# The first block of the input projection: GpSimd's weight remainders start after VectorE's scaling, and the block's products run in three passes

## The chip, the core and the metric

The kernel runs on one core of a Trainium2 chip. The metric is the device time of one execution in microseconds, as the median of the runs. The kernel before takes 1242.05 us (3 runs, 1239.67 to 1242.12).

Five engines work side by side, each through its own list of instructions: TensorE (PE in the profile, its weight loads PEld), VectorE (DVE), ScalarE (ACT), GpSimd (POOL) and SyncE (SP), which here issues most of the DMAs. They wait for each other through semaphores.

## The reference, cut to what matters

One layer of a hybrid backbone runs over 128 context tokens and 256 latent tokens (384 in all). What bears on this case is its start: the modulated RMSNorm and the input projection.

```
h = rmsnorm(x, lp['norm1_w']) * (1 + sc1) + sh1        # (384, 1024); sc1, sh1 from silu(cond) @ w_ada
proj = h @ lp['w_in']                                  # 1024 -> 6496 columns, float32
z_s, xbc, dt_s, qkv, z_d, a_d, b_d = jnp.split(proj, list(np.cumsum(cuts)), axis=-1)
xbc = jax.nn.silu(centred_dwconv(xbc, lp['conv_ssd_w'], lp['conv_ssd_b']))
... # SSD scan, gated delta rule scan, output projection, gated residual
x = x + gt2 * hier_moe(h, lp)                          # 32 experts, top-2 of the top-1 group
```

## The kernel before, in words

Activations lie transposed: `h1_t` holds 8 slices (k = 0 to 7) of 128 features by 392 columns, 384 tokens and 8 columns of padding for the convolution. `KD` is 8.

The projection is made in 50 blocks of 128 output columns. To keep float32 precision, a factor is split in a high part (rounded to fp32r, `w_hi` and `h1_hi`) and a remainder (`w_lo`, `h1_lo`), and a block is the sum of three products for each of 8 slices: w_hi x h1_hi, w_lo x h1_hi, w_hi x h1_lo, 24 matmuls in all.

Who makes what, each engine in the order of its own list:

- ScalarE: `hi_part(n)` (L1122) rounds the weights of block n into `w_split[:, n % 4, 0]`. It makes those of blocks 0, 1 and 2 (`AHEAD` is 3), then the eight slices of `h1_hi` (L1129), each after VectorE has scaled that slice; afterwards the weights of block n + 3 when block n is done.
- GpSimd: for each block, the remainder of the weights, `w_split[:, n % 4, 1]` = weights - `w_hi` (L522), as soon as ScalarE has made the high part.
- VectorE: scales and shifts `h1_t` in place, 16 instructions (L1398: for each slice one of 128 columns, the context tokens, and one of 256, the latent ones), then makes the eight slices of `h1_lo` (L1402) from `h1_t` and `h1_hi`, and then goes on with the convolution of each block that is done (L1410, L1412).
- TensorE: block 0 waits for its weight remainder (`split_ready`) and then, slice by slice, for `h1_lo` (`h1_ready`); each slice has its three matmuls behind each other (L651). Blocks 1 to 49 follow with no wait inside.

The order of the instructions on an engine is the order in which the Python code issues them; there is no scheduler. The weights of block 0 to 3 come by one DMA into the tile `mix`, those of later blocks in halves of `ring_a`. In the profile's names, `kv` is `h1_t` at this point, `h_hi` and `h_lo` are `h1_hi` and `h1_lo`, and `ps` is PSUM. Behind the projection come the scans, the output projection and 16 pairs of experts, whose weight loads SyncE issues when earlier products are done.

Of the kernel before, what the change touches and what calls it, by code (L numbers as in the profile page):

```python
# [7 lines left out]
KD = D_MODEL // P  # L8
# [4 lines left out]
ROW = TOK + 8  # L13
# [46 lines left out]
def hybrid_step(nc, x_t, xs_t, pos_t, params, masks, w_ada, w_in, w_out, h0_ssd, s0_dn, router, final_rows, w_gate, w_up, w_down,  # L60
# [5 lines left out]
    with ctx:  # L66
# [58 lines left out]
        ps = ctx.enter_context(nc.psum_tensor("ps", [P, 8, 512], fp32))  # L125
# [34 lines left out]
        blocks = []  # L160
        for n, (a, w) in enumerate(proj_cols):
            for b in range(w // P):
                i = len(blocks)
# [31 lines left out]
        h1_full = sem("h1_full")  # L195
        h1_hi_ready = sem("h1_hi_ready")
        h1_ready = sem("h1_ready")
        hi_ready = sem("hi_ready")
        split_ready = sem("split_ready")
        block_mm = sem("block_mm")  # L200
# [316 lines left out]
        @block.gpsimd  # L517
        def _(pool):

            for n, (load, c, kind, i) in enumerate(blocks):  # L520
                pool.wait_ge(hi_ready, n + 1)
                nc.gpsimd.tensor_tensor(w_split[:, n % 4, 1, :, :], slots[slot_of[load]][:, :, c:c + P],  # L522
                                        w_split[:, n % 4, 0, :, :].bitcast(fp32), ALU.subtract).then_inc(split_ready, 1)
# [74 lines left out]
        def _(pe):  # L598
# [26 lines left out]
            for k in range(KD):  # L625
                last = nc.tensor.matmul(ps[:, 1, 0:TOK], mask("ones"), v_t[:, k, :], start=(k == 0), stop=(k == KD - 1))
# [10 lines left out]
                nc.tensor.matmul(ps[:, i % 2, 0:TOK], mask("ones"), sq[:, i % 2, :], start=True, stop=True).then_inc(qk_sum, 1)  # L637


            for n, (load, c, kind, i) in enumerate(blocks):  # L640
                pe.wait_ge(split_ready, n + 1)
                if 3 <= n < CONV_BLOCKS + 3:
                    pe.wait_ge(conv_done, n - 2)
                elif n >= 3:
                    pe.wait_ge(block_out, n - 2 - CONV_BLOCKS)
                w_hi, w_lo = w_split[:, n % 4, 0, :, :], w_split[:, n % 4, 1, :, :]
                for k in range(KD):
                    if n == 0:
                        pe.wait_ge(h1_ready, k + 1)
                    for x, (w, h) in enumerate(((w_hi, h1_hi), (w_lo, h1_hi), (w_hi, h1_lo))):  # L650
                        last = nc.tensor.matmul(ps[:, 2 + n % 3, 0:ROW], w[:, k, :], h[:, k, :],  # L651
                                                start=(k == 0 and x == 0), stop=(k == KD - 1 and x == 2))
                last.then_inc(block_mm, 1)
                if n == 9:
                    pe.wait_ge(masks_in, 32)

                    pe.wait_ge(wab_in, 32)
                    for t in range(TT):
                        for k in range(KD):
                            at = ROW_SEGS[min(t, 1)][0] + max(t - 1, 0) * P  # L660
                            last = nc.tensor.matmul(ps[:, 5, 64 * t:64 * t + 64], h1_t[:, k, at:at + P],
                                                    w_ab[:, k, :], start=(k == 0), stop=(k == KD - 1))
                    last.then_inc(tok_mm, 1)
                if kind == "z" and i == 3:

                    pe.wait_ge(log_ready, 1)
                    half_ones = {"first64": mask("ones64")[:, 0:1].to_broadcast([P, P]), "last64": mask("ones64")[:, P - 1:P].to_broadcast([P, P])}
                    for t in range(TT):
                        for m, a, b, o in (("upper", 0, 16, 0), ("lower", 16, 32, 16), ("upper64", 32, 40, 32), ("lower64", 40, 48, 40),
                                           ("ones", 0, 32, 48), ("ones64", 32, 48, 80), ("first64", 32, 48, 96), ("last64", 32, 48, 112)):  # L670
                            last = nc.tensor.matmul(ps[:, 6, t * P + o:t * P + o + b - a], half_ones[m] if m in half_ones else mask(m), g_log[:, t, a:b], start=True, stop=True)
                    last.then_inc(cum_mm, 1)
                if kind == "z" and i:
                    norm_sum(i - 1)
# [92 lines left out]
            for t in range(TT):  # L767
# [4 lines left out]
                for i, src in enumerate((k_t, v_t)):  # L772
                    for b in range(KD):
                        last = nc.tensor.transpose(ps[:, 2 * i + b // 4, (b % 4) * P:(b % 4 + 1) * P], src[:, b, t * P:(t + 1) * P], mask("ident"))
# [122 lines left out]
            for n in range(13):  # L897
# [3 lines left out]
                elif n == 4:  # L901

                    pe.wait_ge(sq_ready, 2)
                    for k in range(KD):
                        last = nc.tensor.matmul(ps[:, 6, 0:TOK], mask("ones"), y_sq[:, k, :], start=(k == 0), stop=(k == KD - 1))
# [63 lines left out]
            for n, k in enumerate((0, 4, 1, 5, 2, 6, 3, 7)):  # L969
                pe.wait_ge(h2_ready[k // 4], k % 4 + 1)  # L970
                for t in range(TT):
                    last = nc.tensor.matmul(ps[:, 5 + t, 0:N_ROUTE], h2_t[:, k, t * P:(t + 1) * P], router_sb[:, k, :],
                                            start=(n == 0), stop=(n == KD - 1))
# [115 lines left out]
        def _(act):  # L1089
# [28 lines left out]
            def hi_part(n):  # L1118
                load, c = blocks[n][:2]
                if c == 0:  # L1120
                    act.wait_ge(slot_in[slot_of[load]], 16 * arrivals(load))
                nc.scalar.copy(w_split[:, n % 4, 0, :, :], slots[slot_of[load]][:, :, c:c + P]).then_inc(hi_ready, 1)  # L1122

            AHEAD = 3
            for n in range(AHEAD):
                hi_part(n)
            for k in range(KD):
                act.wait_ge(h1_full, k + 1)
                nc.scalar.copy(h1_hi[:, k, :], h1_t[:, k, :]).then_inc(h1_hi_ready, 1)  # L1129


            def norm(i):
# [801 lines left out]
```

## Time and profile before

| what | value |
|---|---|
| time, median of 3 runs | 1242.05 us (1239.67 to 1242.12) |
| the profiled execution's own time | 1238.15 us |
| its span | 1236.3 us |
| TensorE busy in the span | 91% |
| VectorE, ScalarE, GpSimd busy | 45%, 24%, 19% |
| mean granted TensorE clock | 0.951 of full |

The span runs from the first to the last instruction. TensorE is busy nearly all the time, with a gap of 12.4 us ahead of the projection's first block. Busy TensorE is not TensorE at full speed: the granted clock counts too (1.00 is 2.4 GHz, 0.50 is 1.2 GHz).

### The profile page before, as it was taken

What the parts mean: (1) busy time and instruction counts of PE and PEld (TensorE: products, weight loads), DVE (VectorE), ACT (ScalarE), POOL (GpSimd) and SP (SyncE); (2) the same over time, 40 slices, a digit from 0 to 9 for tenths busy, and PEclk for the clock granted to TensorE, in tenths of its full rate; (3) what the DMA queues carried; (4) which work ended last, traced back from release to release, by engine and by line L of the source; (5) the groups of instructions that cost most, each with busy time, mean ns of one, the idle gap of its engine ahead of it and who ended that gap; (6) DMA issues with size and microseconds to landing.
All of it is one profiled execution on the core that took longest, in us unless ns stands there. A gap on an engine that the chain in (4) does not pass through costs nothing.

```text
span 1236.3 us, 21464 instructions
## 1 busy us (share of the span) xinstructions
PE 1121.7 (91%) x8981; PEld 736.6 (60%) x8981; DVE 551.6 (45%) x1062; ACT 300.7 (24%) x640; POOL 232.0 (19%) x179
## 2 busy tenths in 40 slices
PE   3599999998697889999899789999999999999996
PEld 1499999997454589999655575333333333333332
DVE  1776776333985356567510341333333222222223
ACT  2333334346221223555200122000000000000002
POOL 0354555341132122222000101000000000000000
PEclk9799999898896999999999759999999999999999
DMA  9632333225024420010400446999999999999993
GB/s 363 216 137 69 136 137 129 75 71 219 18 91 187 171 71 3 4 38 4 154 1 1 202 189 273 425 423 425 426 426 427 424 425 426 425 426 424 424 425 126
DMA packets 52460, 279.20 MB, mean 226 GB/s; under 512 B 6529, under 2 KB 13953, under 8 KB 32929
## 3 DMA queue, kind: packets, MB, share of 16 engines
q1 hardware_dynamic: 49136, 271.66, 54.4%
q0 software_dynamic: 3248, 6.45, 1.5%
q8 instruction: 59, 0.97, 0.3%
q14 instruction: 17, 0.13, 0.0%
HBM read 278.61 MB, written 4.72 MB: 229 GB/s over the span
## 4 chain that ended last, share of the span: by engine, by line
PE 71%; DMA 15%; DVE 9%; ACT 3%; issue 1%; SPq 0%; DVEq 0%; ACTq 0%
PE ps L651 18%; DMA ring_b<-in_w_up 15%; PE ps L1024 14%; PE ps L892 7%; PE ps L1040 5%; PE ps L1054 4%; PE ps L818 3%; PE ps L830 2%; PE ps L827 2%; PE ps L608 2%; DVE temp L1513 1%; DVE temp L1494 1%; PE ps L721 1%; PE ps L741 1%; PE ps L750 1%
## 5 line engine op out<-in xcount | busy, mean ns | idle before, releaser
L651 PE MATMUL ps<-h_hi,w_split 128*128 128x392 f32 x800 | 214.4, 349 | 12.4 <-DVE h_lo L1402 12.4
L651 PEld LDWEIGHTS ps<-h_hi,w_split 128*128 128x128 f32 x800 | 148.5, 190 | 16.7 <-issue 13.2
L651 PE MATMUL ps<-h_lo,w_split 128*128 128x392 f32 x400 | 137.3, 343 | 0.0
L522 POOL TENSOR_TENSOR w_split<-ring_a,w_split 128x1024 fp32r<-128x1024 f32 x46 | 110.8, 2408 | 107.4 <-ACT w_split L1122 107.4
L1040 PE MATMUL ps<-mix,temp 128*64 128x512 f32 x256 | 112.8, 594 | 13.6 <-ACT temp L1343 13.6
L1024 PE MATMUL ps<-ring_b,temp 128*64 128x512 f32 x512 | 113.1, 593 | 7.0 <-DMA ring_b<-in_w_up 7.0
L1024 PE MATMUL ps<-ring_a,temp 128*64 128x512 f32 x512 | 113.4, 595 | 1.2 <-ACT temp L1335 1.2
L1040 PE MATMUL ps<-kv,temp 128*64 128x512 f32 x256 | 113.3, 595 | 0.0
L1054 PE MATMUL ps<-temp 128*128 128x512 f32 x192 | 92.8, 619 | 0.0
L1024 PEld LDWEIGHTS ps<-ring_b,temp 128*64 128x64 f32 x512 | 40.4, 137 | 78.4 <-issue 78.4
L1412 DVE SCALAR_TENSOR_TENSOR temp<-ps,pc,temp 128x388 f32<-128x388 f32 x136 | 84.6, 622 | 4.8
L1024 PEld LDWEIGHTS ps<-ring_a,temp 128*64 128x64 f32 x512 | 35.8, 137 | 76.2 <-issue 76.2
L1122 ACT CAST w_split<-ring_a 128x1024 fp32r<-128x1024 f32 x46 | 48.3, 1049 | 132.4 <-PE ps L651 132.4
L1339 ACT ACTIVATE temp<-ps 128x512 f32<-128x512 f32 x16 | 9.6, 597 | 289.7 <-PE ps L1024 289.7
L1040 PEld LDWEIGHTS ps<-mix,temp 128*64 128x64 f32 x256 | 33.7, 137 | 74.1 <-issue 73.2
L1805 DVE TENSOR_TENSOR x_ssd<-x_ssd,ps 128x512 f32<-128x512 f32 x96 | 66.0, 687 | 25.6 <-PE ps L1054 25.6
L579 POOL DMA_INDIRECT temp<-h_rows,cur_tok x16 | 29.6, 1852 | 247.4 <-PE ps L1014 246.5
L651 PEld LDWEIGHTS ps<-h_lo,w_split 128*128 128x128 f32 x400 | 75.9, 190 | 0.0
L556 POOL TENSOR_TENSOR temp<-bc,masks_sb 128x256 f32<-128x256 f32 x60 | 45.6, 776 | 119.6 <-DVE bc L1563 72.5
L1054 PEld LDWEIGHTS ps<-temp 128*128 128x128 f32 x192 | 29.9, 188 | 62.7 <-DVE x_ssd L1805 41.4
L1796 DVE TENSOR_TENSOR temp<-ps,temp 128x512 f32<-128x512 f32 x32 | 22.1, 692 | 96.6 <-PE ps L1040 96.6
L1578 DVE TENSOR_TENSOR temp<-temp,ps 128x512 f32<-128x512 f32 (+1 forms) x60 | 38.0, 634 | 54.6 <-PE ps L830 54.2
(280 smaller groups left out, 1595.7 us busy)
## 6 DMA issues: line engine op xcount, KB each, us to landing
ring_a<-in_w_gate SPq DMA_DIRECT2D x32, 2048.0 KB, 15.4
ring_b<-in_w_up SPq DMA_DIRECT2D x32, 2048.0 KB, 18.3
kv<-in_w_down SPq DMA_DIRECT2D x32, 1024.0 KB, 21.2
mix<-in_w_down SPq DMA_DIRECT2D x32, 1024.0 KB, 19.2
ring_a<-in_w_in SPq DMA_DIRECT2D x11, 2048.0 KB, 7.7
ring_a<-in_w_ada SPq DMA_DIRECT2D x6, 2048.0 KB, 9.8
ring_b<-in_w_ada SPq DMA_DIRECT2D x6, 2048.0 KB, 18.3
ring_a<-in_w_out SPq DMA_DIRECT2D x2, 2048.0 KB, 14.3
```

Of the source, the lines that this page charges most:

```text
L522: nc.gpsimd.tensor_tensor(w_split[:, n % 4, 1, :, :], slots[slot_of[load]][:, :, c:c + P], w_split[:, n % 4, 0, :, :].bitcast(fp32), ALU.s ...
L556: nc.gpsimd.tensor_tensor(dn_off[a][lev % 2], dn_m[a], mask(f"lev{par}_{LEVELS[lev]}").unsqueeze(1).to_broadcast([P, 4, DN_CHUNK]), ALU.mu ...
L651: last = nc.tensor.matmul(ps[:, 2 + n % 3, 0:ROW], w[:, k, :], h[:, k, :], start=(k == 0 and x == 0), stop=(k == KD - 1 and x == 2))
L818: last = nc.tensor.matmul(A[rows, h, :], off[rows, h, :], mask("eye")[rows, :] if lev == 0 else d[rows, h, :], start=True, stop=True, tile ...
L892: last = nc.tensor.matmul(ps[:, 4 + b % 4, 0:TOK], slots[slot_of[load]][:, k % KD, (b % 4) * P:(b % 4 + 1) * P], mix[:, k, :], start=(k == ...
L1024: last = nc.tensor.matmul(ps[64 * e:64 * e + 64, 2 + n, :], xg_t[:, k, 64 * e:64 * e + 64], slots[2 * n + e][:, k, :], start=(k == 0), sto ...
L1040: last = nc.tensor.matmul(ps[64 * e:64 * e + 64, 5 + n, :], e_act_t[:, f, 64 * e:64 * e + 64], down[4 + e][:, f, n * 512:(n + 1) * 512], s ...
L1054: nc.tensor.matmul(ps[:, (7, 4)[m % 2], :], sel_t[:, t * P:(t + 1) * P], e_y[:, n * 512:(n + 1) * 512], start=True, stop=True).then_inc(sp ...
L1122: nc.scalar.copy(w_split[:, n % 4, 0, :, :], slots[slot_of[load]][:, :, c:c + P]).then_inc(hi_ready, 1)
L1412: ins = V.scalar_tensor_tensor(c_acc, row[:, j:j + W5], col("conv_w", CONV_W * i + j), c_acc, ALU.mult, ALU.add)
L1578: V.tensor_tensor(dn_dd[a][g][:, at:512], dn_dd[a][g][:, at:512], ps[:, a, at:512], ALU.subtract).then_inc(d_ready[a], 1)
L1805: V.tensor_tensor(a, a, ps[:, (7, 4)[m % 2], :], ALU.add).then_inc(acc_added, 1)
```

## The change

Three edits, all around block 0:

1. GpSimd waits for `h1_full` at 8, which VectorE reaches when the last slice is scaled, ahead of its first weight remainder.
2. ScalarE makes `h1_hi` slices 0 to 3, then the high weights of block 0, then slices 4 to 7, then the high weights of blocks 1 and 2.
3. TensorE takes block 0 in three passes over the slices: w_hi x h1_hi, then w_hi x h1_lo, then w_lo x h1_hi. A pass waits for each slice of what it reads (`h1_hi_ready` or `h1_ready`), and the third waits for the remainder of the weights.

```
@@ -517,6 +517,7 @@
         @block.gpsimd
         def _(pool):
 
+            pool.wait_ge(h1_full, KD)
             for n, (load, c, kind, i) in enumerate(blocks):
                 pool.wait_ge(hi_ready, n + 1)
                 nc.gpsimd.tensor_tensor(w_split[:, n % 4, 1, :, :], slots[slot_of[load]][:, :, c:c + P],
@@ -637,7 +638,18 @@
-            for n, (load, c, kind, i) in enumerate(blocks):
+            def first_block():
+                pe.wait_ge(hi_ready, 1)
+                for x, (w, h, made) in enumerate(((0, h1_hi, h1_hi_ready), (0, h1_lo, h1_ready), (1, h1_hi, h1_hi_ready))):
+                    if w:
+                        pe.wait_ge(split_ready, 1)
+                    for k in range(KD):
+                        pe.wait_ge(made, k + 1)
+                        last = nc.tensor.matmul(ps[:, 2, 0:ROW], w_split[:, 0, w, k, :], h[:, k, :], start=(x == 0 and k == 0), stop=(x == 2 and k == KD - 1))
+                last.then_inc(block_mm, 1)
+
+            first_block()
+            for n, (load, c, kind, i) in list(enumerate(blocks))[1:]:
                 pe.wait_ge(split_ready, n + 1)
...
                 for k in range(KD):
-                    if n == 0:
-                        pe.wait_ge(h1_ready, k + 1)
                     for x, (w, h) in enumerate(((w_hi, h1_hi), (w_lo, h1_hi), (w_hi, h1_lo))):
...
             AHEAD = 3
-            for n in range(AHEAD):
-                hi_part(n)
             for k in range(KD):
+                if k == KD // 2:
+                    hi_part(0)
                 act.wait_ge(h1_full, k + 1)
                 nc.scalar.copy(h1_hi[:, k, :], h1_t[:, k, :]).then_inc(h1_hi_ready, 1)
+            for n in range(1, AHEAD):
+                hi_part(n)
```

ScalarE's list from the copy of the modulation row out of PSUM to the first convolved block, before:

```order
L1104 COPY temp<-ps 128x512
L1122 CAST w_split<-mix 128x1024 x3
L1129 CAST h_hi<-kv 128x392 x8
L1122 CAST w_split<-mix 128x1024
L1122 CAST w_split<-ring_a 128x1024
```

And the same stretch of ScalarE's list now (lines shifted; L1132 is the weights, L1139 the activations):

```order
L1114 COPY temp<-ps 128x512
L1139 CAST h_hi<-kv 128x392 x4
L1132 CAST w_split<-mix 128x1024
L1139 CAST h_hi<-kv 128x392 x4
L1132 CAST w_split<-mix 128x1024 x3
L1132 CAST w_split<-ring_a 128x1024
```

Two of the three early weight blocks moved behind all of `h_hi`, and the first one between its halves. The third `mix` cast in the last group of three is that of block 3, which waits for block 0 as before.

TensorE's list with its waits, from the modulation's transposes over the first two slices of block 0, before:

```order
L619 MATMUL ps<-masks_sb,temp 128x128 x3
L651 MATMUL ps<-h_hi,w_split 128x392 [waits h1_ready,split_ready]
L651 MATMUL ps<-h_hi,w_split 128x392
L651 MATMUL ps<-h_lo,w_split 128x392
L651 MATMUL ps<-h_hi,w_split 128x392 [waits h1_ready]
L651 MATMUL ps<-h_hi,w_split 128x392
L651 MATMUL ps<-h_lo,w_split 128x392
```

And now, the whole of block 0 and the start of block 1:

```order
L620 MATMUL ps<-masks_sb,temp 128x128 x3
L648 MATMUL ps<-h_hi,w_split 128x392 [waits h1_hi_ready,hi_ready]
L648 MATMUL ps<-h_hi,w_split 128x392 [waits h1_hi_ready] x7
L648 MATMUL ps<-h_lo,w_split 128x392 [waits h1_ready] x8
L648 MATMUL ps<-h_hi,w_split 128x392 [waits h1_hi_ready,split_ready]
L648 MATMUL ps<-h_hi,w_split 128x392 [waits h1_hi_ready] x7
L661 MATMUL ps<-h_hi,w_split 128x392 [waits split_ready]
```

The 24 matmuls are the same; the wait for the weights' remainder moved behind sixteen of them, and the wait for `h_lo` behind eight.

## Rows read from the trace of the kernel before

**Rows 1.** Chain that ended last, from 34 to 100 us: start us, us, what.
```profile
35.70 0.67 PE ps L619 x4
...
36.97 11.17 DVE kv L1398 x16
48.14 0.48 DVE h_lo L1402
48.62 0.14 issue
48.76 45.02 PE ps L651 x240
```

**Rows 2.** Busy time and granted clock (PEclk) of three stretches, DMA share second last.
```profile
36.97:39.20 2.23, 0.00 (x0) 0.00 (x0) 2.23 (x8) 0.85 (x1) 0.00 (x0) 1.00 1.01 396
...
48.76:52.80 4.04, 4.04 (x12) 4.04 (x13) 3.19 (x7) 0.00 (x0) 0.00 (x0) 0.50 0.41 128
...
59.32:93.70 34.38, 34.38 (x195) 34.38 (x194) 25.37 (x40) 13.93 (x25) 19.32 (x8) 1.00 0.36 123
```

**Rows 3.** VectorE's scaling line: before 39.4 us, 39.6 to 46.8 us, and last three; ns.
```profile
L1398 DVE TENSOR_SCALAR kv<-kv,amp,mod x9: 339/347/409, 37.0 to 39.3; 128x128 f32<-128x128 f32 x5, 128x256 f32<-128x256 f32 x4
...
L1398 DVE TENSOR_SCALAR kv<-kv,amp,mod x4: 339/2509/2580, 39.3 to 44.4; 128x128 f32<-128x128 f32 x2, 128x256 f32<-128x256 f32 x2
...
L1398 DVE TENSOR_SCALAR kv<-kv,amp,mod x3: 335/402/404, 47.2 to 47.7; 128x256 f32<-128x256 f32 x2, 128x128 f32<-128x128 f32 x1
```

**Rows 4.** Timeline, VectorE then GpSimd, around 39.5 us; GpSimd's weight line later.
```profile
39.54 2.58 DVE L1398 TENSOR_SCALAR kv<-kv,amp,mod 128x256 f32<-128x256 f32 x1
...
39.48 7.34 POOL L522 TENSOR_TENSOR w_split<-mix,w_split 128x1024 fp32r<-128x1024 f32 x3 [39.02 <-ACT w_split L1122]
...
L522 POOL TENSOR_TENSOR w_split<-mix,w_split x1: 2413/2413/2413, 56.4 to 56.4; 128x1024 fp32r<-128x1024 f32 x1
```

**Rows 5.** ScalarE's timeline, 15 to 60 us, and VectorE's low parts by line.
```profile
38.35 2.94 ACT L1122 CAST w_split<-mix 128x1024 fp32r<-128x1024 f32 x3 [2.70 <-DMA mix<-in_w_in]
41.20 2.19 ACT L1129 CAST h_hi<-kv 128x392 fp32r<-128x392 f32 x5
...
L1402 DVE TENSOR_TENSOR h_lo<-kv,h_hi x8: 551/552/553, 48.1 to 51.4; 128x392 fp32r<-128x392 f32 x8
```

**Rows 6.** VectorE and GpSimd at 216 to 225 us, and line 1427 later.
```profile
218.10 1.39 DVE L1427 SCALAR_TENSOR_TENSOR q_t<-q_t,temp 128x384 f32<-128x384 f32 x1 [1.78 <-ACT temp L1100]
...
223.03 1.33 DVE L1427 SCALAR_TENSOR_TENSOR q_t<-q_t,temp 128x384 f32<-128x384 f32 x1 [3.06 <-ACT temp L1100]
...
216.68 2.40 POOL L522 TENSOR_TENSOR w_split<-ring_a,w_split 128x1024 fp32r<-128x1024 f32 x1 [2.53 <-ACT w_split L1122]
221.60 2.35 POOL L522 TENSOR_TENSOR w_split<-ring_a,w_split 128x1024 fp32r<-128x1024 f32 x1 [2.52 <-ACT w_split L1122]
...
L1427 DVE SCALAR_TENSOR_TENSOR kv<-kv,temp x8: 557/558/1380, 266.1 to 292.0; 128x384 f32<-128x384 f32 x8
```

**Rows 7.** VectorE's run of L1513 at 340 us, and GpSimd's instruction that began within it.
```profile
340.18 2.44 DVE L1513 SCALAR_TENSOR_TENSOR temp<-temp,gates 128x128 f32<-128x128 f32 x1
...
339.89 2.58 POOL L540 TENSOR_TENSOR temp<-temp,bc 64x1024 f32<-64x1024 f32 x1 [6.56 <-ACT temp L1202]
```

**Rows 8.** VectorE and GpSimd at 698 to 702 us, both with work ready.
```profile
698.28 2.58 DVE L1695 TENSOR_TENSOR buf_h<-q_t,temp 128x1536 f32<-128x1536 f32 x1 [2.80 <-ACT temp L1100]
700.90 0.90 DVE L1698 TENSOR_SCALAR buf_h<-buf_h,amp,mod 128x128 f32<-128x128 f32 x1
...
698.25 0.99 POOL L575 TENSOR_TENSOR buf_h<-q_t,temp 128x384 f32<-128x384 f32 x1 [114.19 <-ACT temp L1100]
699.21 2.51 POOL L575 TENSOR_TENSOR buf_h<-q_t,temp 128x384 f32<-128x384 f32 x1
701.67 0.99 POOL L575 TENSOR_TENSOR buf_h<-q_t,temp 128x384 f32<-128x384 f32 x1
```

**Rows 9.** TensorE's timeline in block 0, and block 1's first pair.
```profile
49.55 0.53 PE L651 MATMUL ps<-h_lo,w_split 128*128 128x392 f32 x1
...
50.53 0.53 PE L651 MATMUL ps<-h_lo,w_split 128*128 128x392 f32 x1
...
53.79 0.34 PE L651 MATMUL ps<-h_lo,w_split 128*128 128x392 f32 x1
...
54.32 0.34 PE L651 MATMUL ps<-h_lo,w_split 128*128 128x392 f32 x1
...
55.04 0.52 PE L651 MATMUL ps<-h_hi,w_split 128*128 128x392 f32 x2
```

## Prediction

> **What bounds the kernel now.** I read the page first for the gap ahead of the projection, then the chain of waits from 34 to 100 us, then the timelines of VectorE, GpSimd and ScalarE in that stretch, and last the places later in the trace where VectorE and GpSimd work at once. The chain [rows 1] shows the whole start of the projection: TensorE ends its transposes at 36.4, then VectorE's sixteen scalings hold the chain for 11.17 us, one `h_lo` follows, and block 0 starts at 48.76. From there to 93.8 TensorE runs 240 matmuls without a gap. So a microsecond taken from ahead of block 1 should be a microsecond of the total: all later work starts from TensorE's progress, and the weight loads are issued on that progress too.
>
> The scalings have two speeds. Nine of them take 339 to 409 ns; three take about 2.5 us, 2.58 the longest; behind these they are at 335 to 404 again [rows 3]. The tenth starts at 39.54 [rows 4], so nine pitches are 2.57 us, 0.286 each. The three slow ones lie exactly over GpSimd's three weight remainders, 39.48 to 46.82 [rows 4]. GpSimd is held hardly at all: 7.34 us for three, and one alone takes 2.41. The two engines exclude each other for a whole instruction, and take turns: one scaling gets in at each change of GpSimd's instruction. Of the 11.17 us about 6.5 are this.
>
> **The change, part by part.** *GpSimd waits.* The scalings then run at their own pitch: the last ends at 36.97 + 15 x 0.286 + 0.40 = 41.66, against 48.14. That is 6.5 us, and nothing else on VectorE moves. If this arrived at block 1 the kernel would gain 6.5 us.
>
> *ScalarE's order.* `h_hi` 0 to 3 follow the scalings (a slice every 0.58) and end near 39.9. One weight cast is 1.04 us and three are 2.94, a pitch of 0.95; five `h_hi` are 2.19 us, a pitch of 0.42 [rows 5]. So `hi_part(0)` ends near 40.9 and its weights had landed by 38.35 [rows 5]; `h_hi` 7 needs the last scaling and ends near 42.5; `hi_part(1)` and `hi_part(2)` end near 43.5 and 44.5. None of these is late for what follows.
>
> *GpSimd's remainders move on to `h_lo`.* This is the step that decides. GpSimd's first remainder now begins at about 41.75, the moment VectorE begins the eight `h_lo`. These take 0.552 us each at a pitch of 0.48 when alone [rows 5], and they read two tensors in SBUF. The trace shows what such an instruction does beside GpSimd: at 218.10 one of 384 columns took 1.39 us and ended 0.41 after GpSimd's instruction (216.68 + 2.40 = 219.08); at 223.03 again, 1.33 us, 0.41 behind 223.95; with GpSimd idle the same form takes 0.557 [rows 6]. A run of them does not keep GpSimd out: at 340.18, in the middle of eight, one took 2.44 us because a GpSimd instruction had begun at 339.89 [rows 7]. And where both have work ready they alternate strictly: GpSimd's at 699.21 took 2.51 instead of 0.99, ending 0.86 after the VectorE instruction (700.86), the next VectorE one ended only at 701.80, and so on [rows 8].
>
> With these numbers: `h_lo` 0 runs 41.59 to 42.14. GpSimd's first remainder, pending, ends about 2.33 later (2.41 alone, less the start already behind it; bounds 2.27 and 2.41), at 44.47; `h_lo` 1 ends 0.42 later, 44.89; second remainder 47.22, `h_lo` 2 47.64; third 49.97, `h_lo` 3 50.39. GpSimd has no fourth until block 0 is done. `h_lo` 4 to 7 follow at 0.477: 52.30. In the trace before only the first `h_lo` was on the path, 0.48 us [rows 1]; now all eight are, for 52.30 - 41.66 = 10.6 us. The 6.5 us that the scaling gives back are taken by `h_lo`, and more.
>
> The Trainium skill has this rule in "SBUF — State Buffer", section "Who interferes with whom": a VectorE instruction with two SBUF inputs contends with a GpSimd one that reads SBUF, although it has no two-port mode, and the later one blocks for the whole instruction. Rows 6 to 8 agree (1.39 against 0.557 us). [...]
>
> *TensorE's three passes.* Alone among the edits this one earns something: in the trace before, all 24 matmuls stand behind `h_lo` 0 and the first remainder; now eight (w_hi x h1_hi) run from about 41 to 43.7, and of the second pass seven run as `h_lo` comes. Behind `h_lo` 7 nine are left: its own and the third pass. The matmuls have two paces: at the granted clock 0.50, the 1.2 GHz level [rows 2], three take 0.98 us (49.55 to 50.53), 0.327 each; at 1.00, 2.4 GHz, three take 0.53, 0.178 each [rows 9]. The first nine after 52.30 + 0.14 (the issue gap, rows 1) = 52.45 take 1.60 us at the higher level and 2.94 at the lower: block 1 would start between 54.05 and 55.4. Before it starts at 55.04 [rows 9]. So the sum for block 1's start is -1.0 to +0.35.
>
> *The clock.* TensorE stood at 0.50 from 48.76 to 52.8 after 12 idle us, and rose after 4.0 us of dense work [rows 2]. Now it has eight matmuls at 41, then one in almost 3 us until 50.4, and dense work from 50.5 (70% busy) or 52.45. If it rises 4.0 us after 50.5, at 54.5, block 1 starts at 52.45 + 9 x 0.178 + 6.3 x 0.149 = 55.0, no change; if it rises 4.0 after 52.45, block 1 starts at 55.4 and about 3 more matmuls cost 0.149 extra, together +0.9. The bounds of this term are -1.0 (never low after 52.45) and +0.9; I take the middle of the two cases with rows behind them, +0.4 us.
>
> *Cover.* The remainders of blocks 1 and 2, now ready at 47.2 and 50.0, are needed at 55 and 59: 5 us to spare. The DMA's share fell from 1.01 to 0.41 ahead of 52.8 [rows 2], so the next weights have landed. Later, GpSimd's remainders meet VectorE's convolution, which has one operand in PSUM, as before. No DMA is moved, and SyncE's waits are the same.
>
> **Sum,** to block 1's start: scaling -6.5; `h_lo` on the path 10.6 instead of 0.5, +10.2; block 0's matmuls on the path 6.3 us before (48.76 to 55.04) and 1.6 to 2.9 now, -4.7 to -3.4; low matmuls behind that, 0 to +0.5. Together -1.0 to +0.9, taken as +0.4, on an execution of 1238.15 us (span 1236.3). The median of the runs is 1242.05, 0.3% above that execution; the difference carries over: 1242.4 us. About 0.2%, 2.5 us, is what a measurement of this kernel can tell from none, so the forecast is no change.
>
> **Rivals.** *A: `h_lo` isn't held.* If these eight, with output in fp32r and 392 columns, run beside GpSimd at their pitch, `h_lo` 7 ends at 41.59 + 3.89 = 45.5; nine matmuls at the lower clock end at 48.6 against 55.04: -6.5, 1235.6 us (-5.6 with a few more low matmuls, -7.8 if the clock has risen). For it: none of the eight overlaps GpSimd in the trace. Against: rows 6 to 8, three forms of VectorE instruction, all held.
>
> *B: VectorE keeps its turn through the eight,* since each begins before the last has ended. Then `h_lo` 7 ends at 45.5, the first remainder at 47.8, the third pass at 50.6; about four low matmuls more: -3.8, 1238.2 us. Against: rows 7, where GpSimd took its turn out of such a run.
>
> *C, slower: the scalings are slow for another reason,* the DMA traffic that fills the stretch. Then they still end at 48.14 with GpSimd waiting, and `h_lo` is held after that, with its last at 58.8: +6.9, 1249.3 us. It decides if scalings without GpSimd are still of 2.5 us. Against: nine ran at 339 to 409 ns while the DMA share was 1.01 [rows 2, 3].
>
> *D, slower: the clock stays low.* Each matmul after 52.45 at 0.50 costs 0.149 more; -1.0 + 0.149 n passes +2.5 at n = 23, a rise as late as 60.0. That wants 7.5 us of dense work without a rise, where the trace before has 4.0.
>
> **Chances.** Forecast 0.77; A 0.08, B 0.06, C 0.04, D 0.05. Faster by over 0.2% 0.14 (A and B), within 0.77, slower 0.09 (C and D). The forecast's own range is 1240 to 1244.5: the clock term -1.0 to +0.9 and the spread of the runs, 2.4. The range that is given reaches just past B, to 1237.8, and above, by D's first part, to 1245; A, C and the rest of D are left out, under 2 in 10.
>
> **What the profile after would show.** Sixteen scalings in about 4.7 us, none over 0.45. Three of the eight `h_lo` at 2.5 to 2.9 us, over GpSimd's three remainders, of which two or three are stretched to about 2.8. TensorE's first matmul near 41, large gaps in the second pass, block 1's first matmul between 54 and 56. The forecast fails if the eight `h_lo` together take under 5 us, or if any scaling takes over 1 us.

## The result and the profile after

The changed kernel takes 1233.5 us as the median of six runs (1230.55 to 1236.02), beside 1240.09 for the kernel before (six runs, 1238.88 to 1242.12): a ratio of 0.9948, 95% interval 0.9932 to 0.9964, some 6.6 us less. The forecast was 1242.4 us and no change; it counted from 1242.05, the median of the first three of the six runs of before, so 2 us of the 8.9 between forecast and measurement are that start.

The chain of the changed kernel that ended last, 34 to 60 us (start us, us, what), stands against [rows 1]:

```profile
36.80 4.73 DVE kv L1410 x16
...
41.54 0.07 issue
...
41.61 5.94 POOL w_split L523
...
47.55 0.04 issue
...
47.60 2.91 PE ps L648 x8
50.51 9.61 PE ps L661 x52
```

The scalings are 4.73 us instead of 11.17, as forecast. Behind them the chain goes to GpSimd, not to `h_lo`, and block 1 starts at 50.3 (its first matmul in TensorE's timeline, 50.31) instead of 55.04. VectorE's timeline of the changed kernel, then GpSimd's (start us, us, engine, line, operation, count), against [rows 3 to 5]:

```profile
41.44 3.90 DVE L1414 TENSOR_TENSOR h_lo<-kv,h_hi 128x392 fp32r<-128x392 f32 x8
50.55 0.68 DVE L1422 TENSOR_SCALAR temp<-ps,pc 128x388 f32<-128x388 f32 x1 [5.21 <-PE ps L648]
...
55.15 0.68 DVE L1422 TENSOR_SCALAR temp<-ps,pc 128x388 f32<-128x388 f32 x1 [1.30 <-PE ps L661]
...
41.61 12.95 POOL L523 TENSOR_TENSOR w_split<-mix,w_split 128x1024 fp32r<-128x1024 f32 x4 [41.15 <-DVE kv L1410]
```

The eight `h_lo` run at their own pace, 3.90 us, and it is GpSimd's first remainder that takes 5.93 us: it ends 2.2 us after the last of all eight (45.34), where alone it takes 2.41. This is the prediction's rival B. TensorE's timeline shows the three passes of block 0, with 1.76 us of waiting for GpSimd ahead of the third:

```profile
40.76 2.98 PE L648 MATMUL ps<-h_hi,w_split 128*128 128x392 f32 x8 [4.57 <-ACT w_split L1132]
43.54 2.31 PE L648 MATMUL ps<-h_lo,w_split 128*128 128x392 f32 x8
47.60 2.91 PE L648 MATMUL ps<-h_hi,w_split 128*128 128x392 f32 x8 [1.76 <-POOL w_split L523]
```

VectorE's second convolution starts when block 1 is done. In the kernel before that is here:

```profile
59.52 0.68 DVE L1410 TENSOR_SCALAR temp<-ps,pc 128x388 f32<-128x388 f32 x1 [0.98 <-PE ps L651]
```

Set to the first scaling, which itself starts up to 1.7 us apart between traces, it comes at 55.15 - 36.80 = 18.35 us against 59.52 - 36.97 = 22.55 before: 4.2 us. The profiled execution as a whole is only 2.4 us shorter (span 1233.9 against 1236.3), since behind block 1 it is 2.0 us longer than that of before; the median is 6.6 us shorter. What lies behind block 1 is told with the repeated run.

### The profile page after: what moved, and what is told of

It is laid out like the page before. It is cut to its first block, busy times and chain, and to the rows that moved or that the text cites. A ratio compares the mean times of both kernels' runs of the same rounds, so it can differ in the third digit from the quotient of the medians.

```text
span 1233.9 us, 21466 instructions
## 1 busy us (share of the span) xinstructions
PE 1127.2 (91%) x8981; PEld 741.9 (60%) x8981; DVE 545.5 (44%) x1062; ACT 300.5 (24%) x640; POOL 234.9 (19%) x179
## 4 chain that ended last, share of the span: by engine, by line
PE 70%; DMA 17%; DVE 7%; ACT 3%; issue 1%; SPq 1%; POOL 0%; DVEq 0%; ACTq 0%
PE ps L661 17%; DMA ring_b<-in_w_up 15%; PE ps L1034 14%; PE ps L902 7%; PE ps L1050 5%; PE ps L1064 4%; PE ps L828 3%; PE ps L840 2%; PE ps L837 2%; DMA ring_b<-in_w_ada 2%; PE ps L731 1%; PE ps L609 1%; PE ps L751 1%; DVE temp L1525 1%; PE ps L760 1%
## 5 line engine op out<-in xcount | busy, mean ns | idle before, releaser
L661 PE MATMUL ps<-h_hi,w_split 128*128 128x392 f32 x784 | 209.7, 349 | 0.0
L661 PEld LDWEIGHTS ps<-h_hi,w_split 128*128 128x128 f32 x784 | 145.3, 190 | 4.0 <-issue 0.6
L661 PE MATMUL ps<-h_lo,w_split 128*128 128x392 f32 x392 | 134.3, 343 | 0.0
L1132 ACT CAST w_split<-ring_a 128x1024 fp32r<-128x1024 f32 x46 | 48.3, 1050 | 134.3 <-PE ps L661 134.3
## 6 DMA issues: line engine op xcount, KB each, us to landing
ring_b<-in_w_ada SPq DMA_DIRECT2D x6, 2048.0 KB, 18.4
```

## The experiments

Each is one version of the changed kernel unless said otherwise. In the table, "block 1 done" is the start of VectorE's second convolution less that of the first scaling, from the trace. A version that ran once has no ratio. "First remainder" is the time of GpSimd's first instruction, its own 2.2 to 2.4 us of work included.

| kernel | eight `h_lo`, us | first remainder, us | block 1 done, us | ratio to before (95%) |
|---|---|---|---|---|
| before | 3.89 | 2.49 | 22.6 | 1 |
| changed | 3.90 | 5.93 | 18.4 | 0.9948 (0.9932 to 0.9964) |
| changed, again | 3.89 | 5.94 | 17.8 | 0.9945 (0.9927 to 0.9963) |
| wait alone | 10.35 | 2.35 | 22.4 | 0.9984 (0.9971 to 0.9998) |
| orders alone | 3.89 | 2.46 | 17.6 | 0.9955 (0.9939 to 0.9972) |
| products as before | 3.90 | 5.93 | 21.0 | 0.9998 (0.9986 to 1.001) |
| wait for seven | 3.89 | 2.54 | 18.5 | one run |
| `h_lo` behind GpSimd | 9.64 | 2.37 | 23.5 | one run |
| VectorE makes the remainder | 3.89 | 1.21 (VectorE) | 15.5 | 0.9941 (0.9921 to 0.9962) |
| the same, again | 3.89 | 1.21 (VectorE) | 14.5 | 0.9927 (0.9911 to 0.9944) |

**The wait alone** (the kernel before with this line):

```
+            pool.wait_ge(h1_full, KD)
             for n, (load, c, kind, i) in enumerate(blocks):
```

> The kernel before with GpSimd's wait alone; ScalarE's and TensorE's orders as before. The changed kernel's trace showed VectorE keeping the ports through all eight h_lo (eight at 0.555 us, GpSimd's first remainder 5.93 us). Theory KEEPS: the same here; h_lo ends near 45.5, the first remainder near 47.8, and TensorE, whose 24 matmuls all stand behind it, starts at 47.9 instead of 48.76: block 1 starts near 54.2 against 55.04, a gain of under 1 us in all. Theory TURNS (the one that the prediction used, if the changed kernel's order was what made the difference): the first remainder ends at 44.5 and three h_lo take 2.5 us or more; block 1 starts near 54 to 55. Both say that the wait alone is worth 0 to 1 us of the 6.5; they differ in the eight h_lo.

Measured: 0.9984. VectorE's `h_lo`, GpSimd's start, and `h_lo` as a group by line (least, median and most of one in ns, then the first and last start):

```profile
41.13 10.35 DVE L1403 TENSOR_TENSOR h_lo<-kv,h_hi 128x392 fp32r<-128x392 f32 x8 [0.17 <-ACT h_hi L1130]
...
41.05 7.62 POOL L523 TENSOR_TENSOR w_split<-mix,w_split 128x1024 fp32r<-128x1024 f32 x3 [40.59 <-DVE kv L1399]
...
L1403 DVE TENSOR_TENSOR h_lo<-kv,h_hi x8: 553/555/2714, 41.1 to 50.9; 128x392 fp32r<-128x392 f32 x8
```

Here the engines do take turns, three `h_lo` at 2.70 to 2.71 us, as in the prediction's sum. Theory TURNS is right for this kernel and KEEPS for the changed one, with the same `h_lo`. The difference that the traces show is who came first: ScalarE makes three weight blocks before `h_hi` here, so VectorE had to wait 0.17 us for `h_hi` 0, and GpSimd began at 41.05, 0.08 ahead of `h_lo` at 41.13. In the changed kernel `h_lo` began at 41.44, GpSimd 0.17 behind it. The last of the experiments on `h_lo` tests this with one wait.

**The orders alone:**

```
-            pool.wait_ge(h1_full, KD)
```

> The changed kernel without GpSimd's wait: both orders stay. The high weights of block 0 are ready at 40.7, so GpSimd's first remainder begins there and ends at 43.1, holding one of the last three scalings for 2.4 us; the second can't start before ScalarE's hi_part(1), near 45. Theory ORDERS: what counts is that ScalarE's order leaves GpSimd nothing to do before 40.7; h_lo runs from 43.9 to 47.8, the third pass ends near 50.5, block 1 starts within 0.5 us of the changed kernel's 50.3, and the time is within 0.2% of the changed kernel's. Theory WAIT: the wait is what brings the gain, and without it the time is back to within 2 us of before.

Measured: 0.9955, median 1232.94 us, not to be told from the changed kernel. GpSimd's timeline:

```profile
40.50 2.46 POOL L523 TENSOR_TENSOR w_split<-mix,w_split 128x1024 fp32r<-128x1024 f32 x1 [40.03 <-ACT w_split L1132]
44.94 9.20 POOL L523 TENSOR_TENSOR w_split<-mix,w_split 128x1024 fp32r<-128x1024 f32 x3 [1.99 <-ACT w_split L1132]
```

The first remainder starts at 40.50 and holds one scaling (2.47 us); the second arrives at 44.94 in the midst of `h_lo`, is kept out, and takes 4.48 us. Theory ORDERS is right: GpSimd's wait, the change's own first edit, brings nothing that can be measured once ScalarE's order gives GpSimd only one block to do early.

**The products as before:**

```
-            first_block()
-            for n, (load, c, kind, i) in list(enumerate(blocks))[1:]:
+            for n, (load, c, kind, i) in enumerate(blocks):
...
                 for k in range(KD):
+                    if n == 0:
+                        pe.wait_ge(h1_ready, k + 1)
```

> GpSimd's wait and ScalarE's order of the changed kernel, with TensorE's order of before: all 24 products of block 0 stand behind h_lo 0 and the first remainder. The first remainder ends at 47.5 as in the changed kernel, TensorE starts at 47.6, with 12 matmuls at the lower clock: block 1 starts near 53.9 against 55.04 before and 50.3 changed. Theory PASSES: two thirds of the gain or more is TensorE's order, so the time is 1 to 1.5 us under before, a ratio of 0.999. Theory SCALING: the scalings' 6.5 us are the gain, and the ratio is 0.995 here too.

Measured: 0.9998. TensorE's first matmuls in this kernel:

```profile
48.75 1.02 PE L652 MATMUL ps<-h_hi,w_split 128*128 128x392 f32 x2 [11.40 <-POOL w_split L523]
```

The scalings and `h_lo` are as quick as in the changed kernel, and it gains nothing that can be measured (block 1 done 1.6 us earlier in the trace, 21.0 against 22.6). TensorE stands idle for 11.4 us until GpSimd's held remainder is done. Theory PASSES is right: TensorE's order, which puts that remainder behind sixteen matmuls, turns the quicker scaling into time. TensorE's order without ScalarE's was not run.

**`h_lo` in four pieces, and by another instruction:**

```
-                V.tensor_tensor(h1_lo[:, k, :], h1_t[:, k, :], h1_hi[:, k, :].bitcast(fp32), ALU.subtract).then_inc(h1_ready, 1)
+                for a in range(0, ROW, ROW // 4):
+                    last = V.tensor_tensor(h1_lo[:, k, a:a + ROW // 4], ..., ALU.subtract)
+                last.then_inc(h1_ready, 1)
```
```
+                V.scalar_tensor_tensor(h1_lo[:, k, :], h1_t[:, k, :], 1.0, h1_hi[:, k, :].bitcast(fp32), ALU.mult, ALU.subtract).then_inc(h1_ready, 1)
```

> The changed kernel with each h_lo made in four pieces of 98 columns. Theory GAP: GpSimd gets its turn only where VectorE leaves the shared ports free for long enough between two instructions; by the pitches of the trace before, an instruction of 392 columns leaves about 0.07 of 0.477 us, the 128-column ones of line 1513 leave 0.13 of 0.263. Pieces of 98 columns should leave 0.13 or more, so GpSimd gets in: its first remainder ends by 44.6, and at least two pieces of h_lo take 2.4 us or more. Theory FORM: a plain TENSOR_TENSOR keeps its turn whatever its width, a SCALAR_TENSOR_TENSOR or a two-speed TENSOR_SCALAR doesn't; then no piece is held and the first remainder takes over 6 us.

> The changed kernel with h_lo made by SCALAR_TENSOR_TENSOR (h1_t x 1.0 - h1_hi), 392 columns as before. Theory FORM: this form yields as in line 1513, so three of the eight take 2.5 us or more, and the first remainder ends by 44.6. Theory GAP: the width is the same, so all eight run at about 0.56 us and the first remainder takes about 5.9 us, as in the changed kernel.

The group by line of VectorE and GpSimd in each, first the four pieces:

```profile
L1415 DVE TENSOR_TENSOR h_lo<-kv,h_hi x32: 251/252/255, 41.6 to 46.9; 128x98 fp32r<-128x98 f32 x32
...
L523 POOL TENSOR_TENSOR w_split<-mix,w_split x1: 7578/7578/7578, 41.7 to 41.7; 128x1024 fp32r<-128x1024 f32 x1
```
```profile
L1414 DVE SCALAR_TENSOR_TENSOR h_lo<-kv,h_hi x8: 554/555/557, 41.1 to 44.4; 128x392 fp32r<-128x392 f32 x8
```

All 32 pieces kept GpSimd out; its first remainder took 7.58 us. The pitch, from one start to the next, was 0.171. How much of a pitch is a gap can be estimated with the two runs that follow: their pitches, 0.538 at 392 columns and 0.231 at 98, give 1.04 ns a column. By that the plain form leaves 0.07 us at 392 columns (0.477) and 0.07 at 98 (0.171): short pieces left no larger gap than long ones, and this run did not test the gap. The other form kept GpSimd out too (first remainder 5.94): theory FORM falls.

**A column as the scalar, at 392 and at 98 columns:**

```
+            dve.wait_ge(masks_in, 16)
...
+                V.scalar_tensor_tensor(h1_lo[:, k, :], h1_t[:, k, :], mask("ones")[:, 0:1], h1_hi[:, k, :].bitcast(fp32), ALU.mult, ALU.subtract).then_inc(h1_ready, 1)
```

> The changed kernel with h_lo made by SCALAR_TENSOR_TENSOR whose scalar is a column in SBUF (of ones), as the instructions of line 1513 have one, instead of the constant 1.0 of the run before. Theory GAP in its mended form: plain and constant forms leave 0.07 us between instructions at any width (pitch 0.477 at 392 columns, 0.171 at 98), a column as scalar adds a gap, as in line 1513 (pitch 0.263 at 128 columns); in that gap GpSimd gets its turn. Then the pitch alone would be near 0.53, GpSimd's first remainder takes under 3.5 us and two or three h_lo take over 2.4. If the eight run at about 0.56 and the first remainder takes about 5.9 us, the scalar is not what lets GpSimd in.

> The changed kernel with h_lo in pieces of 98 columns and a column in SBUF as the scalar: short as the instructions of line 1513, and with the gap that such a scalar adds. So far the run of h_lo kept GpSimd out at 392 columns (plain, constant scalar, column as scalar: pitch 0.477, 0.477, 0.538) and at 98 columns plain (pitch 0.171). Theory SHORT AND GAPPED: GpSimd needs a gap of about 0.13 us and an instruction short beside it, as in line 1513 (pitch 0.263, 128 columns); then the first remainder takes under 3.5 us here and one to three pieces take over 2.2. Theory IN PLACE: line 1513 and the scalings write over what they read, h_lo does not, and that is the difference; then all 32 pieces run at about 0.3 us and the first remainder takes over 9 us.

```profile
L1415 DVE SCALAR_TENSOR_TENSOR h_lo<-kv,masks_sb,h_hi x8: 625/626/628, 41.4 to 45.2; 128x392 fp32r<-128x392 f32 x8
```
```profile
L1416 DVE SCALAR_TENSOR_TENSOR h_lo<-kv,masks_sb,h_hi x32: 309/315/317, 41.7 to 48.9; 128x98 fp32r<-128x98 f32 x32
...
L523 POOL TENSOR_TENSOR w_split<-mix,w_split x1: 9518/9518/9518, 41.9 to 41.9; 128x1024 fp32r<-128x1024 f32 x1
```

By the same estimate the gap rose to 0.13 us in both, that of line 1513 (128 columns, pitch 0.263), and GpSimd was kept out again: its first remainder took 6.41 and 9.52 us. Theories GAP and SHORT AND GAPPED fall. By the second run's own expectation that left IN PLACE, and the next run was for it.

**In place, plain output, and GpSimd in halves.** Three versions on what else sets line 1513 apart, each run once. The first two leave out the remainder of the activations (`h_lo` is set to zero ahead of the scalings), so only the start of their traces counts:

```
+                V.tensor_tensor(h1_lo[:, k, :], h1_lo[:, k, :].bitcast(fp32), h1_hi[:, k, :].bitcast(fp32), ALU.mult).then_inc(h1_ready, 1)
```
```
+                V.tensor_tensor(h1_t[:, k, :], h1_t[:, k, :], h1_hi[:, k, :].bitcast(fp32), ALU.subtract).then_inc(h1_ready, 1)
```
```
+                    for a in (0, 64):
+                        nc.gpsimd.tensor_tensor(w_split[a:a + 64, 0, 1, :, :], ..., ALU.subtract).then_inc(half_done, 1)
+                        pool.wait_ge(half_done, 1 + a // 64)
```

> The changed kernel with each h_lo instruction in place: it multiplies h_lo itself, set to zero ahead of the scalings, by h_hi, 392 columns, two SBUF inputs, output over its first input. It leaves out the remainder of the activations (h_lo stays zero); only the start of the trace is read. Theory IN PLACE: GpSimd gets its turns, three of the eight take 2.5 us or more, the first remainder under 3. Theory SHORT AND GAPPED: the eight run at 0.55 us and the first remainder takes about 5.9.

> The changed kernel with the eight subtractions written over h_t in plain float32, as line 1513 and the scalings write, instead of to h_lo in fp32r. It leaves out the remainder of the activations (h_lo is zeroed) and takes the remainder for h_t in the gate products; only the start of the trace is read. Theory OUTPUT TYPE: GpSimd gets its turns, two or three of the eight take about 2.5 us. Rival: all eight at 0.55, the first remainder at 5.9 us.

> The changed kernel with GpSimd's first remainder in two instructions of 64 partitions, one after the other, since line 540, which got its turn out of a run of VectorE's line 1513, has 64 partitions. Theory FORM OF GPSIMD: the first half gets in within one or two h_lo (one h_lo takes about 2.5 us, the first half under 3.2). Rival: the half is kept out until h_lo is done, 5.9 us, and the eight h_lo run at 0.55; then the partitions are not it.

GpSimd's remainders in the first two as groups by line, and its halves' timeline in the third:

```profile
L523 POOL TENSOR_TENSOR w_split<-mix,w_split x2: 2382/4158/5934, 42.0 to 47.9; 128x1024 fp32r<-128x1024 f32 x2
```
```profile
L523 POOL TENSOR_TENSOR w_split<-mix,w_split x2: 2372/4155/5938, 41.7 to 47.6; 128x1024 fp32r<-128x1024 f32 x2
```
```profile
41.85 8.35 POOL L525 TENSOR_TENSOR w_split<-mix,w_split 64x1024 fp32r<-64x1024 f32 x2 [41.39 <-DVE kv L1417]
```

In all three GpSimd's first instruction took 5.93 to 5.94 us and the eight of VectorE 3.89 or 3.90. IN PLACE, OUTPUT TYPE and FORM OF GPSIMD fall.

**GpSimd waits for seven slices:**

```
-            pool.wait_ge(h1_full, KD)
+            pool.wait_ge(h1_full, KD - 1)
```

> The changed kernel with one number altered: GpSimd waits for seven scaled slices, not eight, so its first remainder begins near 41.0, ahead of the last two scalings and of h_lo. Theory FIRST: who holds the ports when the other comes decides how it goes on. VectorE's unbroken run of h_lo keeps GpSimd out, but once VectorE itself has been held and GpSimd's next remainder is ready behind the first, they take turns, as in the kernel with the wait alone (three h_lo at 2.70 us). Then a scaling takes about 2.5 us, the first remainder about 2.4, and at least two of the scalings or h_lo behind it take over 2 us; block 1 starts at 53 or later against 50.3. Theory LONG RUN: VectorE keeps its turn for any h_lo, and only the one instruction that GpSimd catches is held; then the eight h_lo run at 0.55 us, the second remainder takes over 5 us, and block 1 starts near 50.

```profile
41.96 2.54 POOL L523 TENSOR_TENSOR w_split<-mix,w_split 128x1024 fp32r<-128x1024 f32 x1 [41.50 <-DVE kv L1410]
46.23 9.17 POOL L523 TENSOR_TENSOR w_split<-mix,w_split 128x1024 fp32r<-128x1024 f32 x3 [1.73 <-ACT w_split L1132]
```

GpSimd held the last scaling, but its second remainder was not ready behind the first: ScalarE's `h_hi` 7 had waited for that scaling. It came at 46.23, 1.7 us after VectorE's run had begun, was kept out, and took 4.47. So a VectorE that had just been held keeps its run all the same; the expectation's LONG RUN came out, but its test, a second remainder that waits behind the first, was not made here.

**`h_lo` behind GpSimd's start** made it:

```
+            dve.wait_ge(h1_hi_ready, KD)
             for k in range(KD):
                 dve.wait_ge(h1_hi_ready, k + 1)
```

> The changed kernel with one wait more: VectorE begins h_lo only when all of h_hi is made, at 42.4, when GpSimd has been at its first remainder since 41.7, and the second's input is ready (43.3) before the first ends (44.1). Theory FIRST: behind a GpSimd instruction that began first, with the next one ready, the two take turns, as in the kernel with the wait alone: h_lo 0 ends near 44.5, three of the eight take 1.9 to 2.8 us, the remainders about 2.4, 2.7 and 2.7, the last h_lo ends near 52.3, and block 1 starts near 55, as the prediction had it. Rival LONG RUN: only h_lo 0 is held, the other seven follow at 0.477 and end near 48, the second remainder takes 5 us or more, and block 1 starts near 50.5.

VectorE's and GpSimd's timelines, and the group by line:

```profile
42.44 9.64 DVE L1415 TENSOR_TENSOR h_lo<-kv,h_hi 128x392 fp32r<-128x392 f32 x8 [0.89 <-ACT h_hi L1139]
...
41.64 7.63 POOL L523 TENSOR_TENSOR w_split<-mix,w_split 128x1024 fp32r<-128x1024 f32 x3 [41.17 <-DVE kv L1410]
...
L1415 DVE TENSOR_TENSOR h_lo<-kv,h_hi x8: 552/553/2705, 42.4 to 51.5; 128x392 fp32r<-128x392 f32 x8
```

The turns are back, and with them nearly every number of the prediction: last `h_lo` at 52.08 (predicted 52.30), block 1 from 55.24 (55.0 to 55.4), 1240.67 us beside one run of before at 1241.93. The 52.08 is so near by luck: `h_lo` began 0.85 us later than predicted and took 1.1 us less. One wait of 0.9 us on VectorE takes the gain at block 1 away (23.5 us against 18.4, and 22.6 before).

**VectorE makes the remainder** of block 0, ahead of `h_lo`; GpSimd begins with block 1 once `h_lo` is done:

```
-            pool.wait_ge(h1_full, KD)
-            for n, (load, c, kind, i) in enumerate(blocks):
+            pool.wait_ge(h1_ready, KD)
+            for n, (load, c, kind, i) in list(enumerate(blocks))[1:]:
...
+            passes(0, (hi_hi, lo_hi, hi_lo))
+            passes(1, (hi_hi, hi_lo, lo_hi))
...
+            dve.wait_ge(hi_ready, 1)
+            V.tensor_tensor(w_split[:, 0, 1, :, :], slots[slot_of[LOAD_PROJ]][:, :, 0:P], w_split[:, 0, 0, :, :].bitcast(fp32), ALU.subtract).then_inc(split_ready, 1)
```

> A version meant to beat both. In the changed kernel TensorE waits 1.8 us for the first remainder, which GpSimd could only begin once h_lo was done. Here VectorE makes the remainder of block 0 itself, ahead of h_lo (1024 columns, 1.23 us by line 1379), block 0's passes are w_hi x h_hi, w_lo x h_hi, w_hi x h_lo, GpSimd begins with block 1 once h_lo is done, and block 1 runs in passes too, with its remainder last. Expected: h_lo ends near 46.5, block 1 starts near 47.0 against 50.3, block 1's third pass waits for GpSimd until 48.9 at most, block 2 starts near 51.5 to 52.5 against 55.0: 2 to 3.5 us under the changed kernel, a ratio to before of 0.992 to 0.994. The rival: GpSimd's remainders of blocks 1 and 2 are late (48.9 and 51.3) and TensorE waits for them instead; then block 2 starts at 53 or later and the gain over the changed kernel is under 1 us.

> The version in which VectorE makes block 0's remainder, again, so that it can be set against the changed kernel on the same chip. If its head start holds (block 2 at 51.8 against 54.9 to 55.0), its median is 2 to 3.5 us under the changed kernel's; if the later stages absorb it, the two agree within 1 us.

> The changed kernel itself, beside the version in which VectorE makes block 0's remainder, on the same chip: a ratio of 0.995 to before (0.9932 to 0.9964 so far). Block 1 starts at 50.3 or, where TensorE's clock rises early, at 49.5. What the ratio adds beyond the 4.7 us at block 1 would be chance: from block 1's start to the end the traces so far have 1181.2 us (before), 1183.6 (changed), 1181.2, 1184.6, 1179.3, 1181.7 (the first four experiments), and another of these, between 1179 and 1185, is expected here.

TensorE's timeline in the first run of this version, blocks 0 and 1 and the start of block 2; no wait stands at any of them but the first:

```profile
40.39 5.59 PE L649 MATMUL ps<-h_hi,w_split 128*128 128x392 f32 x16 [4.57 <-ACT w_split L1135]
45.78 1.85 PE L649 MATMUL ps<-h_lo,w_split 128*128 128x392 f32 x8
47.47 1.59 PE L649 MATMUL ps<-h_hi,w_split 128*128 128x392 f32 x8
...
51.76 0.52 PE L664 MATMUL ps<-h_hi,w_split 128*128 128x392 f32 x2
```

Block 1 is done 2.3 to 3.8 us earlier than in the changed kernel (15.5 and 14.5 against 18.4 and 17.8). On the same chip the medians were 1230.71 (six runs, ratio 0.9927, 0.9911 to 0.9944) and 1232.43 for the changed kernel (six runs, 0.9945, 0.9927 to 0.9963). It beats the kernel before clearly. Over the changed kernel the 1.7 us of the medians point the way that the traces do, but the intervals overlap, so the time alone doesn't show that lead, and 1.7 is less than the 2 to 3.5 us that were expected.

The repeated run of the changed kernel says where the rest of the 6.6 us may lie. From "block 1 done" to the end the traces have 1176.7 us (before), 1178.7 (changed), 1174.8 (changed, again), 1180.2 (wait alone), 1176.6 (orders alone), 1178.8 (products as before), 1177.3 and 1181.0 (the last version, twice): a scatter of 6 us in which equal kernels differ by 4. It goes with the granted clock. Behind 60 us the stretches at the lower level add up to 116.5 us in the changed kernel's trace and to 106.3 in its repeat (110.1 before), and over these eight traces more time at the lower level goes with a longer rest almost without exception, 106.3 us with the shortest and 118.1 and 119.6 with the two longest. The times of single runs say the same: the changed kernel's runs of 1230.55, 1233.4 and 1235.77 us had a mean clock of 0.955, 0.952 and 0.949. What the change itself brings is the 4.2 and 4.8 us at block 1 (two traces), beside a measured interval of 4.5 to 8.4 us (0.36% and 0.68% of 1240): the lower of the two lies just below it, the upper within. Of before there is one trace, and over the seven comparisons of medians the gain in time is 0.1 to 2.4 us above the gain at block 1 in six and 1.5 below in one (products as before). That later stages gain anything is not shown.

## Why the prediction was wrong

**The scalings** were right: 4.73 us against 4.7, none slow.

**ScalarE's casts** were right: block 0's high weights at 40.71 (predicted 40.9), `h_hi` 7 at 42.39 (42.5), the next two weight blocks at 43.33 and 44.28 (43.5, 44.5).

**The step that failed** is the one that was called decisive: "A run of them does not keep GpSimd out", and with it the sum by turns, `h_lo` 10.6 us on the path. In the changed kernel the run kept GpSimd out for all eight, and the price moved to GpSimd's first remainder, which ended at 47.54 instead of 44.47. The third pass stands behind it, from 47.60, and block 1 came at 50.3 instead of 54 to 55.4. The readings that fed the step were taken too far. In [rows 8] GpSimd was in first (698.25 against 698.28). In [rows 4] it broke into a run of VectorE that was under way, but a run of scalings, with one input in place, not of `h_lo`. The prediction's own start times, `h_lo` at 41.59 and GpSimd at 41.75, said that here VectorE would be. The two versions in which GpSimd is ahead of the first `h_lo` (wait alone, `h_lo` behind GpSimd) show the turns, 2.63 us each where the prediction had 2.75; the changed kernel and ten variants in which VectorE's run had begun first show none. One wait on VectorE switches between the two, so for `h_lo` the cause is shown, in one run of that version.

**[Rows 7]** was the one piece of evidence for a run with two SBUF inputs that yields. The prediction has it "in the middle of eight"; the whole run is

```profile
338.34 4.28 DVE L1513 SCALAR_TENSOR_TENSOR temp<-temp,gates 128x128 f32<-128x128 f32 x8
```

and ends at 342.62, as the held one does (340.18 + 2.44): it was the last of the eight. The yielding itself is real: in every trace of this study GpSimd's line 540 gets in ahead of the seventh or eighth instruction of this run. It didn't carry over to `h_lo`, and why stays open. Width, form of the instruction, a column as scalar, the gap between instructions, in-place output, output type and the 64 partitions of GpSimd's side were each tried alone (short width and column together) and none is it alone. Not tried were the plain output in place and the repeated input of GpSimd's line 540, and combinations.

**The passes** were costed rightly: from the end of the last wait to block 1 the prediction has 1.6 to 2.9 us for nine matmuls, and the trace 2.71 for eight (47.60 to 50.31). In the sum they only made up for what `h_lo` was to lose; measured, the ratio is 0.9998 without them and 0.9948 with them.

**The cover** was too generous. The remainder of block 1 was to be ready 5 us or more ahead of its use. It was ready at 49.87, 0.4 us ahead; in the repeated run it came too late, and block 1 waited 0.62 us for it:

```profile
47.58 1.71 PE L648 MATMUL ps<-h_hi,w_split 128*128 128x392 f32 x8 [1.25 <-POOL w_split L523]
49.91 0.63 PE L661 MATMUL ps<-h_hi,w_split 128*128 128x392 f32 x2 [0.62 <-POOL w_split L523]
```

**The clock**: after `h_lo` the third pass ran at the lower level (eight matmuls in 2.91 us) in one trace of the changed kernel and at the higher (1.71 us) in the other. In the first the level rose at 44.3, fell again at 47.7 and rose at 51.1, which neither of the prediction's two cases has. Half of the 1.2 us was lost again to the wait for block 1's remainder: block 1 was done 0.6 us apart. The term of -1.0 to +0.9 covers that; it was not what decided. (Its parts add up to +0.8, and D passes +2.5 at 24 matmuls, not 23; neither changes the forecast.)

**Rivals**: B had the mechanism (6 in 100): `h_lo` 7 at 45.5 (measured 45.34), the first remainder at 47.8 (47.54), third pass at 50.6 (50.3), -3.8 us (-4.2 in the trace). Its reason, that each instruction begins before the last has ended, is not shown: those of line 1513 do so too (0.34 us at a pitch of 0.263) and yield. A had `h_lo` 7 right too, but it has GpSimd run beside it; GpSimd was held, and the third pass waited for it. C failed: the scalings ran at 339 to 406 ns beside the same DMA traffic (share 0.95, before 0.98). D did not come: from 51.1 to 218.4 us the level was the higher one. The range was too narrow below because B's price was put at the very edge and the scatter of later stages, some 2 us to either side, was counted for the forecast only; with the median of all six runs of before, 1240.09, B's own number would have been 1236.3.

## What to carry to other kernels

Where VectorE and GpSimd exclude each other, ask not only whether two instructions overlap but which engine is at work as the overlap begins, and whether the other's next instruction is ready behind: with GpSimd 0.08 us ahead of them the eight `h_lo` took 10.35 us, with GpSimd 0.17 us behind 3.90. Look for the same kind of instruction when you do, since the run of scalings and that of line 1513 behaved otherwise. Put on the side that wins what TensorE needs first, and order TensorE's products so that the held operand comes last. A kernel's edits are priced apart: here the wait named first in the change was worth nothing that could be measured once the orders stood (0.9955 without it, 0.9948 with it).

## What the runs showed of the hardware

- The run of `h_lo`, two SBUF inputs each, kept a GpSimd `TENSOR_TENSOR` that came behind its start from ending until 2.2 us after the run's end: it took 5.93 us with 8 of 392 columns, 7.58 with 32 of 98, 9.52 with 32 slower ones, against 2.41 alone. In runs of 32 GpSimd did not get in at any of some 30 borders. The run of line 1513, two SBUF inputs as well, did let GpSimd in.
- With GpSimd first and its next instruction ready, the same VectorE instructions alternated one to one with it, at 2.70 us each instead of 0.55 (wait alone).
- A run of scalings in place by `TENSOR_SCALAR` let GpSimd in at the next border each time (the held one took 2.47 us in the orders alone, 2.60 in the wait for seven).
- The Trainium skill, in "SBUF — State Buffer", section "Who interferes with whom", has that a VectorE instruction with two SBUF inputs contends with a GpSimd one that reads SBUF, and that issue order decides who blocks. The traces agree: 1.39 us against 0.557 in [rows 6], and 10.35 against 3.90 for the eight `h_lo` by who was first.
- Two executions of the same kernel differed by 1.2 us in one pass of eight matmuls by TensorE's granted clock (2.91 against 1.71 us, 0.52 and 1.00 of full).
